# 32-row blocks in 32-column tiles for the levels of a chunked linear attention

## What is computed

```python
bcum = jnp.cumsum(lft, axis=2)                       # log of the forget gates
diff = bcum[:, :, :, None, :] - bcum[:, :, None, :, :]
decay = jnp.exp(jnp.where(causal, diff, -jnp.inf))
attn = jnp.sum(qt[:, :, :, None, :] * kt[:, :, None, :, :] * decay, axis=-1)
```

## Time and profile before

| | us |
|---|---|
| median of 3 runs | 1691.05 (1690.37 to 1692.07) |
| the profiled execution | 1692.61 |
| its span | 1690.6 |
| TensorE matmuls busy | 1354.1 |
| weight loads busy (overlaps) | 764.5 |
| VectorE busy | 333.4 |
| ScalarE busy | 209.4 |

### The profile page before, as it was taken

How to read it: one execution, slowest core, us unless ns; L and a number is a source line. 1 busy time by engine, 2 the same in 40 slices (tenths; PEclk the granted TensorE clock), 3 DMA queues, 4 the chain that set the end, 5 groups by cost and what they waited for, 6 DMA issues and landing times.

```text
span 1690.6 us, 16435 instructions
## 1 busy us (share of the span) xinstructions
PE 1354.1 (80%) x7184; PEld 764.5 (45%) x7184; DVE 333.4 (20%) x597; ACT 209.4 (12%) x372; POOL 1.4 (0%) x6
## 2 busy tenths in 40 slices
PE   6999999999666566656666675666565999999998
PEld 5756997866222122212212221222122445788884
DVE  2135533223101000100100010001001322162222
ACT  1100213102000000000000000000000211134300
POOL 0000000000000000000000000000000000000000
PEclk9999999999988788879878787778888999999999
DMA  7323234357999999999999999999999544424220
GB/s 297 118 106 143 106 116 158 107 232 314 431 430 430 433 433 431 431 430 433 433 430 432 430 433 433 429 433 430 433 432 427 209 183 149 150 100 162 100 100 25
DMA packets 24854, 504.43 MB, mean 298 GB/s; under 512 B 4720, under 2 KB 4976, under 8 KB 6640
## 3 DMA queue, kind: packets, MB, share of 16 engines
q1 hardware_dynamic: 24384, 503.70, 71.4%
q10 hardware_dynamic: 432, 0.17, 0.0%
HBM read 502.81 MB, written 1.05 MB: 298 GB/s over the span
## 4 chain that ended last, share of the span: by engine, by line
PE 53%; DMA 46%; ACT 0%; DVE 0%; issue 0%; SPq 0%; DVEq 0%; ACTq 0%
DMA arena<-in_experts 46%; PE psP L866 37%; PE psP L522 5%; PE psP L533 3%; PE psB L852 1%; PE psB L1137 1%; PE psB L1021 1%; PE psA L1021 1%; PE psA L1103 0%; PE psA L1102 0%; PE psA L852 0%; PE psA L1108 0%; PE psP L924 0%; PE psP L918 0%; DMA X<-in_x 0%
## 5 line engine op out<-in xcount | busy, mean ns | idle before, releaser
L866 PE MATMUL psP<-arena,ring 128*128 128x256 f32 x1600 | 352.5, 382 | 1.4 <-DVE arena L1388 1.4
L866 PEld LDWEIGHTS psP<-arena,ring 128*128 128x128 f32 x1600 | 304.4, 191 | 43.7 <-issue 2.6
L522 PE MATMUL psP<-arena 128*32 128x512 f32 x1024 | 159.5, 780 | 102.3 <-DMA arena<-in_experts 102.3
L522 PE MATMUL psP<-ring,arena 128*32 128x512 f32 x1024 | 155.6, 764 | 104.0 <-DMA ring<-in_experts 104.0
L866 PE MATMUL psP<-ring,arena 128*128 128x512 f32 (+2 forms) x576 | 231.8, 560 | 0.0
L1388 DVE TENSOR_TENSOR X<-X,psA 128x512 f32<-128x512 f32 x66 | 45.4, 688 | 689.5 <-PE psA L543 670.0
L866 PEld LDWEIGHTS psP<-ring,arena 128*128 128x128 f32 x576 | 105.0, 190 | 115.8 <-issue 114.6
L522 PEld LDWEIGHTS psP<-ring,arena 128*32 128x32 f32 x1024 | 40.2, 135 | 217.2 <-issue 174.3
L522 PEld LDWEIGHTS psP<-arena 128*32 128x32 f32 x1024 | 37.5, 138 | 220.9 <-DMA arena<-in_experts 128.6
L533 PE MATMUL psP<-arena 128*32 128x512 f32 x512 | 74.8, 737 | 55.7 <-DMA arena<-in_experts 52.6
L533 PE MATMUL psP<-ring,arena 128*32 128x512 f32 x512 | 72.0, 713 | 51.1 <-DMA ring<-in_experts 49.0
(11 more groups left out here) (247 smaller groups left out, 764.9 us busy)
## 6 DMA issues: line engine op xcount, KB each, us to landing
arena<-in_experts SPq DMA_DIRECT2D x48, 4096.0 KB, 33.3
ring<-in_experts SPq DMA_DIRECT2D x48, 4096.0 KB, 33.3
ring<-in_u_gl SPq DMA_DIRECT2D x6, 2048.0 KB, 7.8
ring<-in_u_hf SPq DMA_DIRECT2D x2, 2048.0 KB, 11.6
ring<-in_u_hq SPq DMA_DIRECT2D x2, 2048.0 KB, 21.8
ring<-in_u_hv SPq DMA_DIRECT2D x2, 2048.0 KB, 7.8
ring<-in_u_hg SPq DMA_DIRECT2D x2, 2048.0 KB, 8.1
ring<-in_u_ga SPq DMA_DIRECT2D x2, 2048.0 KB, 8.0
```

The source lines that it names most:

```text
L522: mm = pe.matmul(z[j * CAP:(j + 1) * CAP, :], x[:, 4 * half + k, j * CAP:(j + 1) * CAP], held[c % 4][:, j, k * 512:(k + 1) * 512], start=( ...
L866: mm = pe.matmul(dsts[o], lhs_of(o, k), rhs_of(o, k), start=(k == 0), stop=(k == kc - 1))
```

## The change

For levels 0 to 7 the matmul of a head is replaced by several that write only the 32-row blocks in which the level's mask has anything. For levels 0 to 5 these are the four blocks 32x32 on the diagonal; for level 6 two blocks 32x32 (keys 0 to 31 by queries 32 to 63, keys 64 to 95 by queries 96 to 127); for level 7 two of 32 keys by 64 queries. The weights are 32 columns of `k`, so a block's rows in PSUM are a column tile of the array; the moving operand is 32 or 64 columns of `q`. Features, 128, stay the contraction. The rest of PSUM keeps what it had, and the mask leaves it out. Nothing else changes: masks, waits, semaphores, the order and the transfers are the same.

```diff
+def level_blocks(n):
+    if n < 6:
+        return [(32 * j, 32 * j, 32) for j in range(4)]
+    if n == 6:
+        return [(64 * j, 64 * j + 32, 32) for j in range(2)]
+    return [(32 * j, 64, 64) for j in range(2)]
...
                             for h in range(HH):
-                                mm = pe.matmul(ps[r][:, h * P:(h + 1) * P], k[:, h, t * P:(t + 1) * P],
-                                               q[:, h, t * P:(t + 1) * P], start=True, stop=True)
+                                for row, col, width in level_blocks(n):
+                                    mm = pe.matmul(ps[r][row:row + 32, h * P + col:h * P + col + width],
+                                                   k[:, h, t * P + row:t * P + row + 32],
+                                                   q[:, h, t * P + col:t * P + col + width], start=True, stop=True)
                             mm.then_inc(full[r], 1)
```

## The result

| | before | after |
|---|---|---|
| median, us | 1690.71 (4 runs) | 1674.94 (1674.16 to 1675.77, 4 runs) |
| profiled execution | 1692.61 | 1675.77 |
| its span | 1690.6 | 1673.7 |

The ratio is 0.9906, 95% interval 0.9891 to 0.9922: 15.8 us less. In a later series on another occasion the same kernel came to 0.9899 (0.9882 to 0.9915). The forecast was 1679.6, in a range of 1673 to 1691.

The account below looks back on a forecast made before the run. TensorE's matmuls were taken to bound the levels, 3.57 us each. Savings of 8.1 us (levels 0 to 5), 2.0 (level 6) and 1.35 (level 7), together 11.4, took the median from 1691.05 to 1679.6; range 1673 to 1691.

Parts of the forecast that it names:

- The bound: Around the levels TensorE alone bounds the path, 3.57 us a level; the experts' transfers come earlier, gain taken whole.
- Four tiles run side by side: In levels 0 to 5, groups of four pairs overlap in four column tiles, as the experts' 128x32 tiles do.
- The price of a group: In the levels: 0.06 us for a group of four, 0.04 at level 6, 0.06 at level 7.
- The burst's 0.007 us a pair: Experts' rows: four pairs in different tiles start within 0.02 us, taken as the low end for feeding.
- the doubling: Levels' pairs priced at 0.015 us, twice the pace of the experts' bursts of four.
- The switches: One way into and one out of the column tiles in each level, together 0.3 us, none between A and B.
- VectorE at the short projection: At the 6.92 us projection, B's copy waits for A's; counted as 0, at most 0.3 us, once.
- The fetch of 640 more pairs: Fetching the levels' added instruction pairs; nothing read priced it, so counted as 0 within the bounds.
- The first rival: Feeding bounds the levels at 0.06 us a pair: +27.6 us, time 1718.7; chance 0.14.
- floor near 0.025 us a pair: Second rival: in the levels a pair costs 0.025 us, tile or not; gain 3.8 us, time 1687.3; chance 0.12.
- VectorE and the transfers took nothing back: Judges the third rival: VectorE or a transfer becomes the bound between levels and later, time 1691; chance 0.04.
- The clock stayed full: Judges the fourth rival: clock falls in projections behind levels, 3 us more a level, time 1704; chance 0.03.

Follow-up runs that it names:

- swapped loops: Changed kernel with the loops over blocks and heads swapped, so 16 pairs in a row use the same column tile; 1688.82 us (one run).
- blocks of 64: Changed kernel with two 64x64 diagonal blocks in 64-column tiles for levels 0 to 5, in place of four of 32x32; 1679.39 us, ratio 0.993.
- With 192 pairs: Changed kernel with only region A of levels 0 to 5 multiplied twice; 1694.98 us (one run).
- with 256: Changed kernel with every level's blocks multiplied twice over; 1714.71 us (one run).
- the runs with stands: Changed kernel with everything multiplied twice, only region A of levels 0 to 5 twice, or only level 2 twice; 1714.71, 1694.98 and 1683.97 us.
- the last version: Changed kernel with latent attention's scores reordered and values' products of the second block's 64-wide attentions alternating between 64-column tiles; 1669.02 us, ratio 0.9862.
- with two blocks: Changed kernel with levels 0 to 5 multiplying only the first two of their four diagonal blocks; 1673.71 us (one run).
- A burst of 256 pairs: Changed kernel with only level 2 multiplied twice over; 1683.97 us (one run).

## Why the prediction was right, step by step

**The bound.** Right. The chain around the levels was TensorE's alone, nothing else took over, and the experts' transfers followed: the wait for them began 17.6 us earlier, of which the span kept 16.9.

**Four tiles run side by side**, read from the experts' rows. Right, with a condition that the prediction didn't name: neighbours in the issue order must lie in different tiles. The swapped loops, with the same pairs, gave back 13 to 14 of 15.8 us. That the edit had the blocks inside the heads, the order that works, was luck as far as the prediction goes: it counts in groups of four tiles, but doesn't ask what another order would do.

**The price of a group**, taken as 0.06 us between 0.03 and 0.24. This is the term that was mis-sized: 0.033, at the lower bound. The burst's 0.007 us a pair was a good guide (0.0083 over 128 pairs) and the doubling "since a level sends 128 pairs in a row" was not needed. The rule that the prediction used for level 7 alone, the moving columns, would have done for all: 0.027 for 32 columns against 0.033 (four tiles) and 0.030 (two), 0.054 for 64 against 0.054 and 0.057 (blocks of 64), 0.107 for 128 against 0.108. Whether the last 0.006 of a group of four is the feeding, whose 4 x 0.0083 is also 0.033, no run separates. Level 6's group was taken as 0.04 and is 0.030; level 7's 0.06 is 0.054. The three together explain the difference: 32 x (6 x 0.027 + 0.010 + 0.006) = 5.7 us too dear.

**The switches**, 0.3 us a level. They are 0.39, 0.7 us in all the other way. 11.4 + 5.7 - 0.7 = 16.4, the levels' saving by the chain; 15.8 was measured, and 16.6 in the later series.

**VectorE at the short projection**, counted as 0. Right. The copy of B now waits for A's and begins at 121.45, the multiplications end at 122.64 + 4.86 = 127.50, and the next level's load follows at 127.81 and is put down to them. But TensorE's loads had stood 0.76 us before it, just as before the level at 104.26, where no engine is waited for, and the projection grew only by the 0.19 of the others (6.92 to 7.11). So nothing is lost.

```profile
121.45 1.29 DVE L1620 COPY_PREDICATED arena<-consts_sb,psB 128x1024 f32<-128x1024 int32 x1
122.64 4.86 DVE L1400 TENSOR_TENSOR arena<-arena 128x1024 f32<-128x1024 f32 x4
```

**The fetch of 640 more pairs, counted as 0.** Right for this kernel, but by luck: the prediction had no reason for the 0, and a level happens to be just one fetched piece, 128 pairs. With 192 pairs the gain of the change was gone, with 256 the kernel was 24 us slower than before it. The first rival, slower by feeding, thus has a real mechanism, but not a steady price a pair: a cliff somewhere between 128 and 192 pairs.

**The rivals.** No floor near 0.025 us a pair was in force across tiles: 128 pairs went at 0.0083 each. Both floors of the Trainium skill, 25 ns from start to start and 62 ns with hardware decode off (TensorE: Matmul & The Clock Gate, "Wait — 56ns, not 53.3ns?"), lie above that, and so do the 60 cycles that the Trainium skill gives each matmul (TensorEngine Tiling (Array Packing), Instruction Overhead; 0.025 us at 2.4 GHz, an estimate). Whether a floor of 0.025 holds inside one tile the swapped loops can't tell: their 0.026 is also the time of the 32 columns. VectorE and the transfers took nothing back. The clock stayed full through the levels of the changed kernel; it fell there only in the runs with stands.

Open: what decides whether the full clock is there at 16 us or only at 22 to 24; what makes an instruction packet come late, and where between 128 and 192 pairs the cliff lies; and where the last 0.5 to 1.4 us of the last version's gain come from. The runs with the blocks doubled, with two blocks and with the swapped loops were executed once each; their stands and levels of microseconds are far above the spread, their totals are good to a microsecond or two.

## What to carry to other kernels

Where a mask uses only blocks on a diagonal, small column tiles pay by the moving columns that they leave out, not by being many; four of 32 columns cost hardly more than two. Price a group of tiles by its moving columns first, at the pace of a large matmul of the same trace. Put neighbours in the issue order into different tiles, and put instructions of the same array form together: a way into and out of the column tiles cost 0.4 us here, and two changes of order alone brought 6.8 us. Count the instructions of a dense burst: up to 128 pairs were free, and with 192 or 256 in a row most levels stood for the next piece of the program.

## What the runs showed of the hardware that was not expected

TensorE's program is fetched in packets of 256 instructions (16 KB). A burst of 256 pairs stood 5.16 us for the next packet, and the clock was at 0.50 from 127.6 to 131.0 us behind it. The profile calls such a stand "issue"; in all 12 of them a packet ended 1.1 to 1.5 us before the engine went on.

With the same work ahead of it, the full clock began at 16 to 17 us in eight executions and at 22 to 24 us in five, and the levels came 1.5 to 3.2 us later in the five.

The same 128 pairs took 1.25 us in four alternating tiles and 3.47 us tile after tile.
